# A product that depends on no activation, moved from the last stage to behind the experts, with three reorderings

## The reference, cut to what matters

```python
h = layer_norm(x, ln_emb_g, ln_emb_b)                  # the embedding norm
...
h = layer_norm(DEEPNORM_ALPHA * h + out, ln1_g[i], ln1_b[i])
gate = jax.nn.sigmoid(jnp.einsum('bld,de->ble', h, w_ple_gate[i]))
ple = jnp.einsum('blq,qd->bld', p[i], w_ple_proj[i])   # p: 1024 x 256, an input
h = layer_norm(DEEPNORM_ALPHA * h + gate * ple, ln2_g[i], ln2_b[i])
```

## Time and profile before

| | |
|---|---|
| median of 3 runs | 2329.94 us (2328.63 to 2330.71) |
| profiled execution | 2331.08 us, span 2329.2 us |
| PE busy | 2118.5 us, 91% of the span |
| DVE, ACT, POOL busy | 1722.0 (74%), 1061.3 (46%), 181.7 us (8%) |
| mean granted clock of TensorE | 0.943 |

### The profile page before, as it was taken

How to read it: one execution, slowest core, us unless ns; L and a number is a source line. 1 busy time by engine, 2 the same in 40 slices (tenths; PEclk the granted TensorE clock), 3 DMA queues, 4 the chain that set the end, 5 groups by cost and what they waited for, 6 DMA issues and landing times. The chain is left out here.

```text
span 2329.2 us, 25516 instructions
## 1 busy us (share of the span) xinstructions
PE 2118.5 (91%) x10156; PEld 1660.1 (71%) x10156; DVE 1722.0 (74%) x1757; ACT 1061.3 (46%) x1194; POOL 181.7 (8%) x154
## 2 busy tenths in 40 slices
PE   5999988999928999999997299999999969899997
PEld 3767835778816888888886278888887757788775
DVE  4575158885576899999995759999999558955727
ACT  4387135882315777777774222122221446522123
POOL 2000010000000111111101200000000000131210
PEclk8999998999958999999999599999999968899999
DMA  9111170002377999999996502212222130332201
GB/s 325 46 37 37 37 285 1 1 1 92 136 305 278 382 394 393 402 394 393 401 394 192 166 2 74 73 37 73 82 91 82 64 119 1 127 118 91 73 1 72
DMA packets 123455, 365.02 MB, mean 157 GB/s; under 512 B 10035, under 2 KB 20683, under 8 KB 123360
## 3 DMA queue, kind: packets, MB, share of 16 engines
q1 hardware_dynamic: 110560, 326.84, 36.8%
q0 software_dynamic: 7568, 23.09, 4.1%
q10 hardware_dynamic: 5232, 13.78, 1.6%
HBM read 324.76 MB, written 38.86 MB: 156 GB/s over the span
## 5 line engine op out<-in xcount | busy, mean ns | idle before, releaser
L2124 DVE SCALAR_TENSOR_TENSOR arena<-arena,vecs 128x1023 f32<-128x1023 f32 (+14 forms) x240 | 304.4, 1268 | 7.1
L1642 DVE TENSOR_TENSOR w_low<-W,w_high 128x2048 fp32r<-128x2048 f32 x96 | 217.0, 2287 | 38.8 <-ACT w_high L1594 38.8
L2021 PE MATMUL Q<-hT_high,w_high 128*128 128x512 f32 (+1 forms) x736 | 227.0, 392 | 5.9 <-DVE ring_low L2167 5.8
L1642 DVE TENSOR_TENSOR w_low<-arena,w_high 128x2048 fp32r<-128x2048 f32 x96 | 218.3, 2290 | 17.7 <-ACT w_high L1594 17.7
L1594 ACT ACTIVATE w_high<-W 128x2048 fp32r<-128x2048 f32 x96 | 184.0, 1919 | 96.1 <-PE Q L1537 65.1
L2021 PE MATMUL Q<-hT_low,w_high 128*128 128x512 f32 (+1 forms) x720 | 222.2, 390 | 0.0
L1594 ACT ACTIVATE w_high<-arena 128x2048 fp32r<-128x2048 f32 x96 | 184.2, 1920 | 74.9 <-PE Q L1537 74.9
L2021 PE MATMUL Q<-hT_high,ring_low 128*128 128x512 f32 x704 | 217.2, 390 | 0.0
L2021 PEld LDWEIGHTS Q<-hT_high,w_high 128*128 128x128 f32 (+1 forms) x736 | 135.5, 184 | 38.9 <-DVE ring_low L2167 5.9
L1537 PE MATMUL Q<-w_high,x_high 128*128 128x512 f32 x512 | 160.6, 395 | 2.4 <-DVE x_low L1645 2.4
L1537 PE MATMUL Q<-w_low,x_high 128*128 128x512 f32 x512 | 158.9, 392 | 0.0
(11 more groups left out here) (449 smaller groups left out, 4267.9 us busy)
## 6 DMA issues: line engine op xcount, KB each, us to landing
W<-in_w_dram SPq DMA_DIRECT2D x48, 2048.0 KB, 12.4
arena<-in_w_dram SPq DMA_DIRECT2D x48, 2048.0 KB, 11.5
W<-in_w_mod_dram SPq DMA_DIRECT2D x12, 2048.0 KB, 14.3
W<-in_w_in_dram SPq DMA_DIRECT2D x12, 2048.0 KB, 8.3
W<-in_w_out_dram SPq DMA_DIRECT2D x6, 2048.0 KB, 12.5
spill<-arena ACTq DMA_DIRECT2D x24, 512.0 KB, 2.6
W<-in_w_in_dram SPq DMA_DIRECT2D x8, 1024.0 KB, 7.7
arena<-in_x_dram SPq DMA_DIRECT2D x4, 1024.0 KB, 17.5
```

What stands on the lines that cost most here:

```text
L1642: nc.vector.tensor_tensor(wl[:], chunk_src(r, j), wh[:].bitcast(F32), ALU.subtract).then_inc(low_v, 1)
L2021: ins = nc.tensor.matmul(Q[rows, 2 * (n % 4) + half, :], w[:, k], x[:, k, HALF * half:HALF * half + HALF], start=k == 0 and w is high and ...
L2124: ins = nc.vector.scalar_tensor_tensor(conf[:, i, j:], u[:, 0:S - j], w, conf[:, i, j:], ALU.mult, ALU.add)
```

## The change

It has four parts. (1) Product of p. p, its weights and the row of the embedding norm's gain are loaded behind the weights of the last expert (SyncE waits for the low part of expert 15's last chunk), the row of its bias two chunks later. TensorE turns p behind the turn of h, ScalarE copies it, and the 16 products are made in full precision, eight behind the last expert product and eight at the start of the embedding norm. ScalarE copies each to one of six staging halves and stores it to a DRAM buffer, ple_rows. In the last stage the rows are loaded in three pieces and VectorE reads them from SBUF. (2) The last expert's `turned_h` stands ahead of `outputs(E - 2)`, and its last product goes to banks 0 and 1. (3) The gates' order is (0,0), (0,1), (0,2), (1,0), (0,3), (1,1), ... (0,7), (1,5), (1,6), (1,7); `unit_high_part(5)` stands ahead of the late tiles' high parts; the last norm's statistics are made for each half when it is ready; the root of a tile comes right behind its own sigmoid. (4) In the norm of q and k, `added(3)` stands ahead of the second reciprocal, `low_rows(1)` ahead of `norm(1)`, and the near copies and `y_rest` ahead of `added(1)`; ScalarE's order follows.

The changed lines are shown without the lines around them, and their indentation within a piece is cut.

```diff
@@ -61,6 +61,7 @@
+ple_rows = dram("ple_rows", (S, D))
@@ -939,6 +940,9 @@
+act.wait_ge(near_mm, HEADS)
+for m in range(2):
+    nc.scalar.activation(y_high[m][:], y_lru[:, m], ACT.Copy).then_inc(ylru_high_ready, 1)
@@ -950,10 +954,8 @@
-for m in range(2):
-    nc.scalar.activation(y_high[m][:], y_lru[:, m], ACT.Copy).then_inc(ylru_high_ready, 1)
+high_rows(1)
-high_rows(1)
@@ -988,11 +990,13 @@
-dve.wait_ge(mod_in, 4 * 16)
-added(0)
+dve.wait_ge(mod_in, 4 * 16)
+added(0)
+for m in range(2):
+    y_rest(dve, m)
@@ -1003,19 +1007,16 @@
+added(3)
-added(3)
-norm(1)
-norm(2)
-norm(3)
+for n in range(1, HEADS):
+    norm(n)
-for m in range(2):
-    y_rest(dve, m)
@@ -1499,6 +1500,39 @@
+PLE_EARLY, PLE_SLOTS = NT, 6
+p_sb, w_ple, pT = tiles(26, NT, 256), tiles(28, 2), tiles(30, 2)
+ple_stage = [tiles(t)[:, HALF * j:HALF * j + HALF] for t in (34, 35, 36) for j in range(2)]
...
+def ple_bank(i):
+    return 2 + i % 6 if i < PLE_EARLY else 4 + i % 4
+def ple(pe, i):
+    t, n = divmod(i, 2)
+    for k in range(2):
+        ins = nc.tensor.matmul(Q[:, ple_bank(i), :], pT[:, k, P * t:P * t + P],
+                               w_ple[:, k, HALF * n:HALF * n + HALF], start=k == 0, stop=k == 1)
+    ins.then_inc(ple_mm, 1)
+def keep_ple(act, i):
+    t, n = divmod(i, 2)
+    j = i % PLE_SLOTS
+    act.wait_ge(ple_mm, i + 1)
+    if i >= PLE_SLOTS:
+        act.wait_ge(ple_stored[j], 16 * (i // PLE_SLOTS))
+    nc.scalar.activation(ple_stage[j], Q[:, ple_bank(i), :], ACT.Copy).then_inc(ple_kept, 1)
+    act.wait_ge(ple_kept, i + 1)
+    act.dma_start(ple_rows[P * t:P * t + P, HALF * n:HALF * n + HALF], ple_stage[j])\
+        .then_inc(ple_stored[j], 16)
@@ -1510,7 +1544,13 @@
+sync.wait_ge(*low_level(E - 1, CPE - 1))
+sync.dma_start(p_sb, A["p_2"][0, 0].rearrange("(t p) q -> p t q", p=P)).then_inc(p_in, 16)
+sync.dma_start(w_ple, A["w_ple_proj_2"][0].rearrange("(k p) n -> p k n", p=P)).then_inc(w_ple_in, 16)
+sync.dma_start(emb_g, bc_row(A["ln_emb_g_2"], D)).then_inc(vec_in, 16)
+sync.wait_ge(*low_level(E, 1))
+sync.dma_start(emb_b, bc_row(A["ln_emb_b_2"], D)).then_inc(vec_in, 16)
@@ -1576,10 +1616,23 @@
+pe.wait_ge(p_in, 16)
+for j in range(2):
+    for t in range(NT):
+        ins = nc.tensor.transpose(Q[:, 2 * j + t // 4, P * (t % 4):P * (t % 4) + P],
+                                  p_sb[:, t, P * j:P * j + P], ident[:])
+ins.then_inc(p_tr, 1)
+pe.wait_ge(pT_ready, 1)
+for j in range(4):
+    product(E, j, 0, h_high, h_low)
+pe.wait_ge(w_ple_in, 16)
+pe.wait_ge(pT_ready, 2)
-for j in range(4):
-    product(E, j, 4, h_high, h_low)
+for i in range(PLE_EARLY):
+    if i >= 6:
+        pe.wait_ge(ple_kept, i - 5)
+    ple(pe, i)
@@ -1633,6 +1686,13 @@
+act.wait_ge(*low_level(E, 1))
+act.wait_ge(p_tr, 1)
+for j in range(2):
+    nc.scalar.activation(pT[:, j], bank2(j), ACT.Copy).then_inc(pT_ready, 1)
+act.wait_ge(*low_level(E, 3))
+for i in range(PLE_EARLY):
+    keep_ple(act, i)
@@ -1663,13 +1723,13 @@
...
-    nc.vector.scalar_tensor_tensor(y_e, bank2(2), gate, GATE2, ALU.mult, ALU.mult)\
+    nc.vector.scalar_tensor_tensor(y_e, bank2(pair), gate, GATE2, ALU.mult, ALU.mult)\
@@ -1702,9 +1762,9 @@
+turned_h(E - 1)
-turned_h(E - 1)
-outputs(E - 1)
+outputs(E - 1, pair=0)
...
@@ -1795,14 +1854,15 @@
-act.dma_start(emb_g, bc_row(A["ln_emb_g_2"], D)).then_inc(vec_in, 16)
-act.dma_start(emb_b, bc_row(A["ln_emb_b_2"], D)).then_inc(vec_in, 16)
-root(0)
+for i in range(PLE_EARLY, 2 * NT):
+    keep_ple(act, i)
+    if i == 2 * NT - 4:
+        root(0)
@@ -1810,9 +1870,15 @@
+for j in range(PLE_SLOTS):
+    act.wait_ge(ple_stored[j], 16 * len(range(j, 2 * NT, PLE_SLOTS)))
+for i in range(PLE_EARLY, 2 * NT):
+    if i >= PLE_EARLY + 4:
+        pe.wait_ge(ple_kept, i - 3)
+    ple(pe, i)
@@ -1822,6 +1888,7 @@
+pe.wait_ge(ple_kept, 2 * NT)
@@ -1857,6 +1924,8 @@
+if t == 1:
+    dve.wait_ge(ple_mm, 2 * NT)
@@ -2473,21 +2542,26 @@
...
+ple_at = [tiles(8, 12, HALF)[:, (NT * n + t) % 12] for n in range(2) for t in range(NT)]
+bn2 = router_w[:].rearrange("p k e -> p (k e)")[:, 0:12 * NT].rearrange("p (t s) -> p t s", t=NT)
...
+GATE_LAG = 2
+g_order = [(n, t) for q in range(NT + GATE_LAG) for n, t in ((0, q), (1, q - GATE_LAG)) if 0 <= t < NT]
@@ -2505,7 +2579,7 @@
-used_at[U_PLE + n] = (gate_mm, NT * (n + 1))
+used_at[U_PLE + n] = (gate_mm, g_order.index((n, NT - 1)) + 1)
@@ -2533,11 +2607,14 @@
-sync.dma_start(p_sb, A["p_2"][0, 0].rearrange("(t p) q -> p t q", p=P)).then_inc(p_in, 16)
-sync.dma_start(w_ple, A["w_ple_proj_2"][0].rearrange("(k p) n -> p k n", p=P)).then_inc(tail_in, 16)
+ple_of = ple_rows.rearrange("(t p) d -> p t d", p=P)
+sync.dma_start(tiles(8, NT, HALF), ple_of[:, :, 0:HALF]).then_inc(ple_in[0], 16)
+sync.dma_start(tiles(12, 4, HALF), ple_of[:, 0:4, HALF:]).then_inc(ple_in[1], 16)
+sync.wait_ge(ple_read, g_order.index((0, 3)) + 1)
+sync.dma_start(tiles(8, 4, HALF), ple_of[:, 4:NT, HALF:]).then_inc(ple_in[2], 16)
@@ -2603,8 +2680,7 @@
-def gate(i):
-    n, t = divmod(i, NT)
+for i, (n, t) in enumerate(g_order):
@@ -2612,36 +2688,8 @@
-def ple(i):
-    n, t = divmod(i, NT)
-    if i >= 4:
-        pe.wait_ge(ple_read, i - 3)
-    for k in range(2):
-        ins = nc.tensor.matmul(Q[:, i % 4, :], pT[:, k, P * t:P * t + P],
-                               w_ple[:, k, HALF * n:HALF * n + HALF], start=k == 0, stop=k == 1)
-    ins.then_inc(ple_mm, 1)
-for i in range(4):
-    gate(i)
-pe.wait_ge(p_in, 16)
-pe.wait_ge(h1T_low_ready, NT)
-for j in range(2):
-    for t in range(NT):
-        ins = nc.tensor.transpose(Q[:, 2 * j + t // 4, P * (t % 4):P * (t % 4) + P],
-                                  p_sb[:, t, P * j:P * j + P], ident[:])
-ins.then_inc(p_tr, 1)
-gate(4)
-pe.wait_ge(tail_in, 48)
-pe.wait_ge(pT_ready, 2)
-for i in range(4):
-    ple(i)
-for i in range(4, 2 * NT):
-    if i > 4:
-        gate(i)
-    ple(i)
@@ -2690,22 +2738,16 @@
+unit_high_part(5)
-for i in range(2 * NT):
-    if i == 2:
-        act.wait_ge(p_tr, 1)
-        for j in range(2):
-            nc.scalar.activation(pT[:, j], bank2(j), ACT.Copy).then_inc(pT_ready, 1)
-    if i == NT // 2:
-        unit_high_part(5)
+for i, (n, t) in enumerate(g_order):
-    if i > NT:
-        root_2(act, i - NT - 1)
-root_2(act, NT - 1)
+    if n == 1:
+        root_2(act, t)
@@ -2810,21 +2852,28 @@
-for n in range(2):
-    for t in range(NT):
-        i, half = NT * n + t, slice(HALF * n, HALF * n + HALF)
-        g = gate_sb[i % 2][:, 0:HALF]
-        dve.wait_ge(gate_ready, i + 1)
-        dve.wait_ge(ple_mm, i + 1)
-        nc.vector.tensor_tensor(g, g, Q[:, i % 4, :], ALU.mult).then_inc(ple_mult, 1)
-        dve.wait_ge(ple_mult, i + 1)
-        nc.vector.scalar_tensor_tensor(res[:, t, half], res[:, t, half], ALPHA, g, ALU.mult, ALU.add)\
-            .then_inc(ple_read, 1)
-        if n == 1:
-            dve.wait_ge(ple_read, i + 1)
-            if t == 0:
-                dve.wait_ge(tail_in, 48)
-            normed(t, ln2_g, ln2_b, var2, root2_, out_ready)
+for i, (n, t) in enumerate(g_order):
+    half, g = slice(HALF * n, HALF * n + HALF), gate_sb[i % 2][:, 0:HALF]
+    if t in (0, 4):
+        dve.wait_ge(ple_in[0 if n == 0 else 1 + t // 4], 16)
+    dve.wait_ge(gate_ready, i + 1)
+    nc.vector.tensor_tensor(g, g, ple_at[NT * n + t], ALU.mult).then_inc(ple_mult, 1)
+    dve.wait_ge(ple_mult, i + 1)
+    nc.vector.scalar_tensor_tensor(res[:, t, half], res[:, t, half], ALPHA, g, ALU.mult, ALU.add)\
+        .then_inc(ple_read, 1)
+    dve.wait_ge(ple_read, i + 1)
+    v_link(nc.vector.bn_stats(bn2[:, t, 6 * n:6 * n + 6], res[:, t, half]))
+    if n == 1:
+        nc.vector.bn_aggr(mv[:, 0:2], bn2[:, t]).then_inc(var2, 1)
+        if t == 0:
+            dve.wait_ge(tail_in, 32)
+        dve.wait_ge(root2_, t + 1)
+        dve.wait_ge(var2, t + 1)
+        v_link(nc.vector.reciprocal(rstd[:, t:t + 1], rstd[:, t:t + 1]))
+        v_link(nc.vector.scalar_tensor_tensor(res[:, t], res[:, t], mv[:, 0:1], ln2_g,
+                                              ALU.subtract, ALU.mult))
+        nc.vector.scalar_tensor_tensor(res[:, t], res[:, t], rstd[:, t:t + 1], ln2_b,
+                                       ALU.mult, ALU.add).then_inc(out_ready, 1)
```

More of the change, by code:

```diff
@@ L1501, in program @@
             used_at[U_MOE + u] = (moe_mm, 2 * u + 2)
+        PLE_EARLY, PLE_SLOTS = NT, 6
+        p_sb, w_ple, pT = tiles(26, NT, 256), tiles(28, 2), tiles(30, 2)
+        ple_stage = [tiles(t)[:, HALF * j:HALF * j + HALF] for t in (34, 35, 36) for j in range(2)]
+        p_in, w_ple_in, p_tr, pT_ready = sem("p_in"), sem("w_ple_in"), sem("p_tr"), sem("pT_ready")
+        ple_mm, ple_kept = sem("ple_mm", kept=True), sem("ple_kept", kept=True)
+        ple_stored = [sem(f"ple_stored{j}", kept=True) for j in range(PLE_SLOTS)]
+        emb_g, emb_b = tiles(12), tiles(33)
+        vec_in = sem("vec_in", kept=True)
+        def ple_bank(i):
[16 more added lines that the diff above has]
+                .then_inc(ple_stored[j], 16)
         with nc.Block() as block:
@@ L1664, in hidden, with outputs @@
```

(18 more changed lines are left out.)

## The result

The changed kernel takes 2303.38 us (median of 4 runs, 2300.77 to 2305.21) against 2330.32 of the kernel before (4 runs, 2328.63 to 2330.83): ratio 0.9883, 95% interval 0.9872 to 0.9895, 27 us less. The forecast said 38.6 less, 2291.4, in a range of 2288 to 2298. Direction and the large term came; 11.6 us of the gain didn't. The profiled run took 2304.0 us (span 2302.3, mean granted clock 0.946).

A forecast was written before the change was run, and what follows sets the result against it. Bounds: TensorE's gates with p's products, then a serial tail; VectorE in the q and k norm; TensorE idle between experts and embedding norm. -27.5 - 5.3 - 6.6 + 0.8 = -38.6, from 2329.94 to 2291.4, range 2288 to 2298.

The forecast's parts named there:

- Step 1: Last stretch: gates without p's turn and 15 products of p between them, 27.5 us less.
- D: Last stretch: the fourth gate stands for its weights, 2 to 6 us, total 2293 to 2297; chance 0.05.
- E: Last stretch: a late unit 5 stops turns, gates and sigmoids, slower than before, 2342 at 60 us landing; chance 0.02.
- Step 2: From the last gate to the last pass: 6.13 us instead of 11.43, 5.3 us less.
- Rival C: Gates and end: a drain behind each table load makes ScalarE slower, 1.9 us more, total 2293.3; chance 0.04.
- Step 3: Norm of q and k: VectorE's new order removes waits, 6.6 us less, bounds 7.5 and 3.2.
- Rival B: Norm of q and k: new order gives its lower bound or nothing, through transfers or clock, 2295 to 2298; chance 0.09.
- Step 4: Experts' end and embedding norm: 0.5 us later, then 0.3 later, 0.8 us more; bounds -0.5 and +6.
- behind that VectorE sets the pace as before: Embedding norm after its first turn at 14.1 us: VectorE's pace unchanged, tiles having 4 us of slack at the second.
- rival A: Boundary of experts and embedding norm: lower clock (2.4), p or tiles late (2 to 3), total 2296; chance 0.13.

The follow-up runs named there:

- the statistics experiment: The changed kernel with both statistics instructions of the last norm behind the second half, not by halves: 2303.97 us, 0.9889 of the kernel before.
- early roots: The changed kernel with the embedding norm's first roots and turn earlier, last two stores behind root 2, low parts one tile later: 2293.42 us, 0.9841 of the kernel before.

## Why the prediction was wrong, step by step

- **Step 1, gates: right.** From the end of gate 0 to that of gate 15: 2314.42 - 2202.00 = 112.42 before, 2292.83 - 2208.49 = 84.34 after, so 28.1 less, forecast 27.5. The rest is 0.05 us on each of 15 gates (5.45 in place of 5.50). No gate behind the first waited for weights: GpSimd's second unit took 11.8 us, not 13.7, against the earlier trace rows. Rivals D and E didn't occur.
- **Step 2, the end: right.** 6.34 against 6.13, 5.1 less than before instead of 5.3. The 0.2 more is backlog: the last three tiles follow each other on VectorE without a wait (the chain), not one alone as forecast; the statistics experiment, with three times 0.6, confirms it. Rival C fell: 0.02 us after a table load the next ScalarE instruction begins (1295.46 + 1.28 = 1296.74, then 1296.76), and the load of the last tile begins 0.01 us behind the sigmoid (2292.86 + 0.60, then 2293.47). The drain that the Trainium skill adds to each load (ScalarE: Activation LUTs, "What ACT_TABLE_LOAD costs") is not in these traces; the measurement decides.
- **Step 3, norm of q and k: the term was mis-sized, 6.6 forecast, 2.5 measured on the sum.** VectorE's list was right: its stretch gained 6.0 against the old order on the same kernel, and 6.3 (58.1 to 51.8) between two traces in which the clock doesn't fall at 317 us. What the forecast lacked is the clock in two places. A fall of 3.4 us inside the sums costs 1.7; and the attention, for which the sum has no term, stands at 1.2 GHz for 14.0 and 16.9 us at its start instead of for 4.5. That cost 3.3 and 4.6 us in the changed kernel's two traces, and between 0 and 4.6 in all seven of the new order without extra products. The forecast asked for the clock at the experts' end and not here, though the earlier trace rows showed a product at the lower one. Rival B had this size and named the clock as one of two possible takers, though inside the norm and not in the attention behind it.
- **Step 4, boundary: the experts' part right, the embedding norm's wrong.** TensorE's hole was 2.85 us (2.8 forecast), the clock stayed at 1.0 (in two later traces it fell here), the product began at 1257.74 and p's first at 1268.75; +0.6 against +0.5. In the norm the first pass came at 11.8 (11.45). The step that failed is "behind that VectorE sets the pace as before": it priced every issue of a store at 0.4 us, and of the shared DMA it said only that the tiles have slack. Two issues took 5.08 us together (5.68 in the second trace), and the second root stood behind them. Measured +3.9; rival A named the place and, with 2296, the size, but its causes were late tiles, which were on time, and the clock at the experts' end, which held.
- **Sum.** Embedding norm 3.6, attention 3.3, the q and k norm's own stretch 2.0, code not touched 3.3 (of it the second projection 1.2: TensorE starts it at 0.50 for 7 us before, for 9 after), experts 0.1, less 0.7 of the last stretch: 11.6. The 3.3 of untouched code (the time ahead of the first stretch, both projections, the scan) can be chance of a run: the same parts together differ by 3.3 between the two traces of the kernel before and by 3.5 between those of the changed one. The range failed because its high side, 2298, held rivals A and B one at a time; both together, 4.6 and 3.6 to 6.6 us, come to 2299.6 to 2302.6, and losses of both sizes came about.

## What to carry over

An instruction that issues a DMA belongs to its engine's path, at the price that it has while other transfers are under way (here up to 3.3 us and not 0.33): when a list mixes small roots that others wait for with stores that nobody does, put the roots first. A gain in front of a stretch that begins with holes is checked in that stretch too, since TensorE's clock can take it back there; read the sum of both, over several traces. And where several independent losses are each likely, the range has to hold two of them at once.

## What the runs showed of the hardware

- A 256 KB store's issue took ScalarE 0.33 to 0.36 us for the first six behind the barrier, and 3.27 and 1.81 us for the next two (3.18 and 2.50, 2.38 and 1.91 in other traces) with 4 MB of loads asked for at the barrier; with 1.5 MB, 0.95 and 0.33. The number of stores alone doesn't decide: in one trace the fourth and fifth took 2.57 and 3.30.
- The granted clock can fall amid dense work: in the changed kernel TensorE was busy for all of the 3.4 us before 317.7 us, and the clock fell there for 3.4 (6.8 in three other traces). The fall is missing in one trace of the same code (early roots), in two with extra products and in one of the kernel before. Its cause is open.
- Products whose results nobody reads held the clock through the norm's holes: with them it was at 1.00 from 323 us to the attention's start in all seven traces, and on to the attention's end in five. Without them it was at 0.50 for 27 us between 345 and 376 in the changed kernel.
